# Two fused transformer blocks in float32: the side work of retention, of differential attention and of the second block's key and query moves stands at other units

## The reference, cut to what matters

```python
def reference(x, ...):
    x = first_block(x, ...)
    return second_block(x, p_2, ...)

def first_block(x, ...):
    for l in range(2):
        h = x @ w_in[l]
        rq, rk, rv, rg, cq, ck, cv, dq, dk, dv, gates = split(h)
        o_a = _retention(rq, rk, rv, rg, ret_norm_g[l])          # rotary on rq and rk, gate rg
        o_b = _chunk_attention(cq, ck, cv, ca_rel_bias[l])
        o_c = _diff_attention(dq, dk, dv, lam, lambda_init, da_norm_g[l])   # rotary on dq and dk
        g = sigmoid(gates + b_merge[l])
        merged = g0 * (o_a @ w_branch_a[l]) + g1 * (o_b @ w_branch_b[l]) + g2 * (o_c @ w_branch_c[l])
        x = layer_norm(ALPHA * x + merged @ w_out[l])
        x = layer_norm(ALPHA * x + ffn(x))

def hybrid_layer(h, ...):
    h = h + 0.5 * swiglu(rmsnorm(h))
    z = rmsnorm(h) @ w_in                      # m_qk, m_v, m_o, m_i, m_f, a_q, a_k, a_v, g_m, g_a
    m_q, m_k = split(silu(causal_dwconv(m_qk)))
    hm = sigmoid(m_o) * head_rmsnorm(mlstm_chunkwise(m_q, m_k, m_v, ...))
    ha = swa_gqa_sinks(head_rmsnorm(a_q), head_rmsnorm(a_k), a_v, a_sinks)
    h = h + (sigmoid(g_m) * (hm @ w_branch_m) + sigmoid(g_a) * (ha @ w_branch_a)) @ w_out
    h = h + 0.5 * swiglu(rmsnorm(h))
    return h + sigmoid(rmsnorm(h) @ ple_gate_w) * (p_i @ ple_proj_w)
```

## Time and profile before

| | |
|---|---|
| median of three runs | 2307.84 us |
| the profiled execution's own time | 2307.95 us |
| its span in the trace | 2306.2 us |
| TensorE matmuls busy | 2283.7 us (99%), granted clock 0.998 in the mean |
| VectorE busy | 1527.7 us (66%) |
| ScalarE busy | 1233.8 us (53%) |
| GpSimd busy | 128.6 us (6%) |
| DMA | 483.08 MB, mean 209 GB/s |

### The profile page before, as it was taken

How to read it: one execution, slowest core, us unless ns; L and a number is a source line. 1 busy time by engine, 2 the same in 40 slices (tenths; PEclk the granted TensorE clock), 3 DMA queues, 4 the chain that set the end, 5 groups by cost and what they waited for, 6 DMA issues and landing times.

```text
span 2306.2 us, 30120 instructions
## 1 busy us (share of the span) xinstructions
PE 2283.7 (99%) x11144; PEld 1906.6 (83%) x11144; DVE 1527.7 (66%) x2411; ACT 1233.8 (53%) x1890; POOL 128.6 (6%) x141
## 2 busy tenths in 40 slices
PE   9999999999999999999999999999999999999999
PEld 8887888888878888888878888888888888888887
DVE  6656786566567866576587765664766587657654
ACT  6555544445555454354467654554554478555543
POOL 3140000004300000000000000000000000000000
PEclk9999999999999999999999999999999999999999
DMA  8556568756475587577564444875677564456772
GB/s 336 199 192 238 190 220 290 228 185 214 156 267 186 172 287 242 180 256 248 189 230 157 157 155 165 265 241 195 219 244 238 178 215 156 150 171 209 233 235 89
DMA packets 179857, 483.08 MB, mean 209 GB/s; under 512 B 20480, under 2 KB 65152, under 8 KB 178688
## 3 DMA queue, kind: packets, MB, share of 16 engines
q1 hardware_dynamic: 179712, 481.16, 61.7%
HBM read 452.24 MB, written 28.84 MB: 209 GB/s over the span
## 4 chain that ended last, share of the span: by engine, by line
PE 92%; DVE 3%; DMA 3%; ACT 1%; SPq 1%; issue 1%; POOL 0%; DVEq 0%; ACTq 0%
PE bank L2104 27%; PE bank L2109 27%; PE bank L2108 27%; PE bank L2151 2%; PE bank L2091 2%; PE bank L2092 2%; PE bank L2093 2%; DMA raw<-in_weights 1%; DVE wl L1593 1%; PE bank L2240 1%; SPq L1181 1%; DMA rg<-moved 1%; DMA moved<-rv 0%; PE bank L2202 0%; PE bank L2225 0%
## 5 line engine op out<-in xcount | busy, mean ns | idle before, releaser
L1363 ACT ACTIVATE wh<-raw 128x1024 fp32r<-128x1024 f32 (+1 forms) x778 | 814.5, 1051 | 768.1 <-PE bank L2109 690.8
L1593 DVE TENSOR_TENSOR wl<-raw,wh 128x1024 fp32r<-128x1024 f32 (+1 forms) x778 | 927.8, 1223 | 282.9 <-ACT wh L1363 279.3
L2104 PE MATMUL bank<-wh,xh 128*128 128x512 f32 (+1 forms) x2102 | 826.8, 393 | 5.0 <-issue 3.9
L2109 PE MATMUL bank<-wh,xl 128*128 128x512 f32 (+1 forms) x2102 | 816.8, 389 | 0.0
L2108 PE MATMUL bank<-wl,xh 128*128 128x512 f32 (+1 forms) x2102 | 815.7, 388 | 0.0
L2104 PEld LDWEIGHTS bank<-wh,xh 128*128 128x128 f32 x2102 | 395.2, 188 | 87.0 <-issue 7.3
L2109 PEld LDWEIGHTS bank<-wh,xl 128*128 128x128 f32 x2102 | 394.9, 188 | 81.0
L2108 PEld LDWEIGHTS bank<-wl,xh 128*128 128x128 f32 x2102 | 395.5, 188 | 76.9
L2104 PE MATMUL bank<-wh,act_h 128*128 128x512 f32 x528 | 206.0, 390 | 0.0
L2109 PE MATMUL bank<-wh,act_l 128*128 128x512 f32 x512 | 199.4, 389 | 0.0
L2108 PE MATMUL bank<-wl,act_h 128*128 128x512 f32 x512 | 199.3, 389 | 0.0
(11 more groups left out here) (347 smaller groups left out, 2066.9 us busy)
## 6 DMA issues: line engine op xcount, KB each, us to landing
raw<-in_weights SPq DMA_DIRECT2D x760, 512.0 KB, 4.3
turn<-ffn_s SPq DMA_DIRECT2D x264, 64.0 KB, 2.8
ffn_a<-turn SPq DMA_DIRECT2D x66, 256.0 KB, 4.7
raw<-in_weights SPq DMA_DIRECT2D x16, 384.0 KB, 3.2
ln<-in_ln SPq DMA_DIRECT2D x4, 1024.0 KB, 6.8
moved<-merged SPq DMA_DIRECT2D x32, 128.0 KB, 3.5
merged<-moved SPq DMA_DIRECT2D x8, 512.0 KB, 7.0
bias<-in_bias SPq DMA_DIRECT2D x2, 1024.0 KB, 9.3
```

The lines of the kernel that those rows point to most:

```text
L1363: act.activation(wh[:, u % NH, 0:used(u)], raw[:, u % NR, 0:used(u)], ACT.Copy).then_inc(hi_done, 1)
L1593: dve.tensor_tensor(wl[:, u % NR, 0:used(u)], raw[:, u % NR, 0:used(u)], wh[:, u % NH, 0:used(u)].bitcast(F32), ALU.subtract).then_inc(lo_ ...
L2104: pe.matmul(out, h, w_h, start=st.first and i == 0, stop=False)
L2109: last = pe.matmul(out, lo, w_h, start=False, stop=ends)
```

## The change: what it does

It changes the two tables and the place of some moves; no operation is added or removed, and sizes and engines stay.

In the first block all of retention stands three to five units further up. The copies of rq and rk stand behind units 34 and 35 (before: 37 and 39), the four heads' `ret_s` and `ret_pv` behind units 37 to 41 (before: 41 to 46), `ret_fin` behind 41 (before: 46), "block" of rg and the two loads bm12 and ln1 behind 42 (before: 47), "out" of rg behind 43 and 44 (48 and 49), "block" of dq and dk behind 45 (49), "back" of rg behind 46 and 47 (50 and 51), "out" of dq and dk behind 47 and 48 (51 and 52), "halve" of rg behind 49 and 50 (52 and 53), "back" of dq and dk behind 50 and 51 (53 and 54), their copies behind 53 and 54 (56 and 57). Differential attention follows three units earlier, from its first scores behind unit 57 (60) to the move of its result `oc`, whose "halve" stands behind 79 (81). The keep and rope of dk stay behind unit 43. Layer 1 has the same table.

In the second block "out" of ak and aq0 stand among aq1's units (`OUT_EARLY`), "back" of ak ahead of the narrow unit, "back" of aq0 and "out" of aq1 behind it, and only the copies and "back" of aq1 among the convolved units. The diff:

```diff
+OUT_EARLY = {1: "ak", 2: "aq0"}
 OUT_AT, BACK_AT, LAST_AT = 0, 2, 4
...
-UNITS_AMONG_1 = "0101110101110001100001010111322201001101000110011010101213311002101010201102232"
+UNITS_AMONG_1 = "0101110101110001100001010111012101001101000111011011101213311002101010201102244"
...
+    def out_early(i):
+        if i in OUT_EARLY:
+            p.moved("out", OUT_EARLY[i])
+
     def kept_rows(name, c0, dst, off, pair):
-        c = p.chunk(("w_in", [(c0, c0 + 512)]), "x", KT, 512, pair, t_x)
+        c = p.chunk(("w_in", [(c0, c0 + 512)]), "x", KT, 512, pair, t_x, among=out_early if name == "aq1" else None)
...
             p.moved("block", name, kept=q[name])
+    p.moved("back", "ak")
...
     p.add("m_narrow", c=c_log)
+    p.moved("back", "aq0")
+    p.moved("out", "aq1")
...
-    for what in ("out", "back", "copy"):
-        for name in ("ak", "aq0", "aq1"):
-            c_a = p.moved(what, name)
+    for name in ("ak", "aq0", "aq1"):
+        if name == "aq1":
+            p.moved("back", name)
+        c_a = p.moved("copy", name)
```

More of the change, by code:

```diff
@@ L30 @@
 NH = 10
+OUT_EARLY = {1: "ak", 2: "aq0"}
 OUT_AT, BACK_AT, LAST_AT = 0, 2, 4
 WARM = (3, 3)
-UNITS_AMONG_1 = "0101110101110001100001010111322201001101000110011010101213311002101010201102232"
-UNITS_AMONG_2 = "10000020101100011211002110001101011110011110401001111100100111101101000101020040102"
+UNITS_AMONG_1 = "0101110101110001100001010111012101001101000111011011101213311002101010201102244"
+UNITS_AMONG_2 = "100110300011211002110001101011110011110401001111100100111101101000101020040102"
 TAILS = {"branch_c": (4, 1, 2, 3), "w_out_1": (8, 6, 5, 5), "ffn_1": (10, 5, 4, 6), "branch_m": (8, 5, 3, 5),
```

## The result

The changed kernel takes 2315.07 us in the median of six runs (2313.34 to 2318.3), the kernel before 2307.07 us in six (2304.26 to 2308.96). The ratio is 1.0036, with a 95% interval from 1.0023 to 1.0049: 8.3 us slower, between 5.3 and 11.3. The forecast was 2316.8 us, that is +8.9. The profiled execution took 2314.7 us, its span is 2313.0 (before 2306.2).

What follows compares the result with a forecast made beforehand. TensorE, busy 2283.7 of 2306.2 us, was taken as the bound, so only its idle time and half clock could change. Layer 0 +4.8, layer 1 +5.5 and second block -1.4 gave +8.9 on 2307.95: 2316.8 us, range 2301 to 2327.

Steps and rivals of the forecast that it cites:

- The rope: GpSimd's rope of dk in layer 0: to start at 150.9, take 13.3 us like dq's, and end at 164.2.
- Part 2: Weight 57 lands late behind 3.67 MB at 0.362 MB/us; TensorE waits 6.8 us before unit 52, plus 1.6 of half clock.
- The half clock: TensorE's slow clock behind the new wait before unit 52, put at 1.6 us.
- A and B: TensorE's old waits for `oa_l` in layers 0 and 1, costing 6.2 and 5.5 us with half clock; expected to go.
- Part 3: Differential attention's first scores wait 2.6 us more for the copy of dk's transpose, with no second clock drop charged.
- the rival with 0.418: Transfers at 0.418 MB/us: first wait 5.5 + 1.6 us, scores find their copy; 2309.1 us in total; chance 0.24.
- Part 4: Second block: the wait for `aqT` goes, -1.4 us; the waits of 1.97 us stay, their half clock 0 within 1.6.
- -1.4 us: Second block: the wait of 1.41 us for `aqT` disappears.
- the 1.97 us: Second block's two layers: one TensorE wait of 1.97 us each, ending with VectorE's convolution, expected unchanged.
- The faster one: Rival: the wait for the ropes holds nothing TensorE misses; -13.1 us, 2294.9 us; chance 0.13.
- The cascade: Rival: ropes end at 166.8, transfers at 0.321 MB/us, dk's copy 5.2 us late; +22.1 us, 2330 us; chance 0.08.
- The ceiling itself: Fabric limit of 435 GB/s: at it the new wait would be 5.1 us, the next vanish, and the sum show no change.

Runs made afterwards that it cites:

- table1: The kernel before with only the first block's changed table (UNITS_AMONG_1); 2317.14 us against 2306.66, ratio 1.0051.
- wait_only: The changed kernel, but behind unit 42 SP only waits for the ropes; bm12 and ln1 load behind the back of dk; 2324.39 us in one run.
- loads_up: The kernel before with only the loads bm12 and ln1 moved up, behind unit 42; 2322.85 us in one run.
- moves2: The changed kernel with the old first-block table, so only the second block's moves stand earlier; 2302.34 us against 2307.24, ratio 0.9978.
- moves2b: The same kernel as moves2, run again; 2303.59 us against 2306.69, ratio 0.9987.
- loads_far: The changed kernel with bm12 moved from behind unit 42 to behind unit 56, and ln1 to behind unit 63; 2294.43 us against 2306.66, ratio 0.9948.
- sums_late: loads_far with the two a_sum steps one unit further down in the second block; 2298.7 us.

## Why the prediction was right, point by point

- **The mechanism** was the predicted one at every link: unit 43's end (149.3 forecast, 149.50 measured), the rope's start (150.9; 151.21) and end (164.2; 164.53), SP standing until then, weight 57 behind 2.1 MB of loads, dv's copy behind weight 57 (177.6 for its end; 178.85), TensorE idle before unit 52 (from 171.16, and in layer 1 from 659.05, where 653 was forecast without the 4.8 us that layer 0 adds). The changed kernel's 2315.07 us lie 1.7 below the forecast 2316.8.
- **The rope.** dk's rope took 13.32 us, dq's length of 13.3. Three of its operations ran at 1.60 us, all beside a `wl` (VectorE computed three from 155.21 to 160.17), and the first at 2.40 us, beside the last product of ret_fin and a `wl`; the rest took 0.74. That GpSimd contends with VectorE's instructions of two SBUF inputs, as the Trainium skill says (GPSIMD Engine Reference, Specifications), fits this: a `wl` and a product of ret_fin read two tensors from SBUF each. That page gives no price; here an operation took two to three times as long. The transposes of rg, which the prediction counted among the hindrances, cost nothing: the three operations from 153.57 on ran beside them at 0.74 to 0.75. dq's rope had four slow operations of 1.61 to 1.77 us and one of 1.21, so that the two lengths agree is in part luck.
- **Part 2, mis-sized.** The first wait was put at 6.8 us and was 7.78 and 8.20. Weight 57 was rounded 12.3 us after the rope's end, where 11.3 were worked out. The rate was the term: 324 GB/s from 164.6 to 176.8, near the lower bound of 0.321 MB/us and not at 0.362.
- **The half clock, mis-sized.** I put the price that A and B had paid, 1.6 us, behind the new wait; it was 3.0 and 2.9. In table1 the same waits (7.79 and 7.99 us) paid 2.0 and 2.4, so a range would have been the right term.
- **Part 3, wrong.** The wait of 2.6 us for `kT` did not come, for two reasons. The scores stood only at 198.30, since the first stop and its half clock were 2.4 us longer than forecast (1.0 and 1.4), and 198.3 is when the forecast had the copy ready: a longer first wait eats the second. And the copy itself began at 195.27 instead of 197.2, so it was ready 2 us early. By the prediction's own reckoning the 11.0 MB went at some 0.39 MB/us instead of 0.362: slower up to weight 57, as above, and 408 to 417 GB/s in the stretches from 180 to 195. The average that I had taken fitted neither part, and the rival with 0.418 was right in this second one. So 10.8 and 11.1 us for each layer stand beside the forecast 11.0, but the forecast's sum was set by the copy of dk and the measured one by the first stop and its clock. That they agree so closely is luck.
- **Part 4.** -1.4 us came, and the 1.97 us stayed, as forecast.
- **The rivals.** The faster one needed the ropes done by 157.6; they were by 164.53. The cascade's later rope did not come. Its step, a second wait behind a late queue, did in wait_only.
- **The rates.** The row at 164 us (418 GB/s) already spoke against 358 GB/s as a limit for a core that runs alone (the Trainium skill, DMA: Bandwidth & Descriptors, Specifications); in the changed kernel the stretches of 1 us from 179 to 186 moved 380 to 423 GB/s, below its ceiling of 435. The ceiling itself as a rate for the whole backlog would have put the wait at 5.1 us, too short. The prediction is wrong in calling 418 the fastest full microsecond: the stretch from 165 to 166 in the kernel before reads 451 GB/s, at a DMA share of 1.09. A share above one shows that single stretches of 1 us are rough; longer ones carry the argument better.

## What to carry to other kernels

A step that waits must not be moved up along with its neighbours: ask of each what it waits for, and what stands behind it in its queue. Here two loads that could be issued 21 and 43 us later without anyone waiting for them (185.30 and 207.87 against 164.62 and 164.99) turned a change worth -12 us into +8. In these runs loads_up was missed by following a late weight to one row behind it and not to the others: follow a late item through every row behind it on its engine; and when a wait is shortened, look where its transfers go, since on a queue that is nearly full they come back at the next deadline.

## What the runs showed of the hardware

**The clock behind a stop.** What a stop cost in half clock did not follow its length. All prices are the extra time of the matmuls behind the restart against those at full clock. Stops of 4.35, 3.85 and 2.54 us (before; moves2) cost 1.7 us each, one of 4.01 us (moves2b, layer 0) 2.8. Stops of 7.79 and 7.99 us (table1) cost 2.0 and 2.4, of 7.78 and 8.20 us (the changed kernel) 3.0 and 2.9, of 11.63 and 11.47 us (loads_up) 3.0 and 1.5. In wait_only one of 3.35 us cost 1.5 and one of 3.24 us nothing. In the long stops the granted clock had fallen before the restart (at about 175 in the changed kernel's layer 0), and the part of the low stretch that lies in the stop costs nothing. Waits of the same 1.97 us were followed by the half clock in some executions (both layers of loads_far) and not in others (neither of moves2). Six waits of 1.4 to 1.6 us in sums_late cost no clock, nor did waits of under half a microsecond, of which each trace has several.

**GpSimd beside VectorE.** A GpSimd product of two 128 x 256 tensors took 0.74 us alone or beside a transpose, 1.60 beside a `wl` and 2.40 beside a product of ret_fin and a `wl` (the changed kernel, 151.21 to 164.53).
